# First mixer's attention: the multiplication of the softmax moves from VectorE to ScalarE

## The chip, the cores and the metric

The kernel runs on one NeuronCore of a Trainium2 chip. The metric is the device time of one execution in microseconds. The core has five engines that run their own instruction streams and wait for each other by semaphores: TensorE (PE; its weight loads are listed as PEld), VectorE (DVE), ScalarE (ACT), GpSimd (POOL) and SyncE (SP, which issues the transfers).

## The reference, cut to what matters

Two layers of an encoder, 256 tokens of 1024 channels, in float32. Each layer is a half-step SwiGLU block, a mixer, and another half-step SwiGLU block. The first layer's mixer projects the tokens once into 18 tiles of 128 channels: 12 go to a convolution branch (short convolution, gate, long convolution by Fourier transforms), 6 to a windowed attention with 8 query heads of 64 channels and 2 key/value heads. The attention's softmax has a sink logit in the denominator:

```
s = q @ k^T * D**-0.5 - slope * |distance|, masked outside the band
m = max(max(s), sink)
p = exp(s - m)
p = p / (sum(p) + exp(sink - m))
o = p @ v
```

Both branches are concatenated and go through one output projection. The second layer's mixer is a bidirectional RWKV-7 scan; it is not touched by the change.

## The kernel before, in words

Activations are kept channel-major: 128 channels on the partitions, 256 tokens along the free axis. All weights come as one stream of steps of three blocks of 128x1024, loaded by SyncE into two raw buffers. Each step is split into a high and a low part: ScalarE makes the high part (L187 and L193, `next_hi`), VectorE the low part of the first two blocks (L199, `next_lo`) and GpSimd that of the last block (L208). A product is three TensorE matmuls (L244 to L246).

The first mixer (`pe_mix0`, `act_mix0`, `dve_mix0`) is a hand-written loop over j = 0 to 17, one projected tile each. The order in which an engine's work stands in its own loop body is the order in which it runs; nothing is scheduled by a planner. Below, "step j" is one pass of that loop. A projected tile is brought out of PSUM by VectorE (L1099, `evacuate`); ScalarE then starts its short convolution (L1062) or squares it, and VectorE finishes the convolution in the next step (L1105 and L1107, `conv`). From j = 9 to 16 the attention runs beside it, one head per step, head h = j - 9:

- VectorE, `biased`: adds the distance bias to the scores (L1130), takes the row maximum (L1133) and its negative (L1135, which releases ScalarE);
- ScalarE, `exps`: two exponentials of 128x256, one per half of the queries, each with its row sum (L1028), and the exponential of the sink (L1029, which releases VectorE);
- VectorE, `shares`: the sum (L1140), its reciprocal (L1142), and the two multiplications of the exponentials by it (L1145, into the tile SC, which releases TensorE);
- TensorE, `probs`: four transposes of the shares (L895); ScalarE copies them out of PSUM (L1023) in the next step; TensorE multiplies them with the values for two heads at a time (L909), ScalarE copies the result (L1033) and VectorE makes its low part (L1150).

TensorE's own order in a step is: projection of tile j, for odd j from 11 the product with the values, the scores (L886: heads 0 and 1 in steps 8 and 9, then two heads at a time in steps 10, 12 and 14), the transposes of head j - 9, and for j = 9, 11, 13, 15 the transposes of a gated tile (L918). The scores of head 1 use a swapped copy of the keys, which ScalarE makes in step 9 (L1049). ScalarE's order in a step is: L1023, `exps`, then the step's single copies (L1049 or L1053), in steps 9, 12 and 15 the high part of the next weights (L187, L193), in odd steps from 11 the copy L1033, and last L1062. VectorE's order is: in even steps from 12 L1150, `biased`, `conv` of tile j - 1, `shares`, in steps 10, 13 and 16 the low part of the next weights (L199), and `evacuate` of tile j. GpSimd makes the low part of the third block and the gates of the convolution branch (L1941). After the transposes of the last head (step 16) TensorE does the two Fourier transforms (L925), the last projection and the output projection.

Of the kernel before, what the change touches and what calls it, by code (L numbers as in the profile page):

```python
# [95 lines left out]
def build(nc, io):  # L96
    fp32 = mybir.dt.float32
    f32r = mybir.dt.float32r
    ALU = mybir.AluOpType
    ACT = mybir.ActivationFunctionType  # L100
# [3 lines left out]
    with ctx:  # L104
# [3 lines left out]
        def sem(name):  # L108
            return ctx.enter_context(nc.semaphore(name))
# [33 lines left out]
        def pcol(name, i=0):  # L143
            return par[:, COL[name] + i:COL[name] + i + 1]
# [80 lines left out]
        def next_hi(act, s):  # L225
            if s < STEPS:
                split_hi(act, s)
# [157 lines left out]
        def act_squares(act):  # L385
            for a, b in ((0, 4), (4, 6), (6, 8)):
                nc.scalar.activation(XSQ[:, a:b, :], X[:, a:b, :], ACT.Square).then_inc(sq_ready, 1)

        def act_sqrt_table(act):
            nc.scalar.activation(small[:, 61:62], eps6[:, 0:1], ACT.Sqrt)  # L390
# [37 lines left out]
        def act_root(act, n):  # L428
            act.wait_ge(st_ready, n + 1)
            if n == 0:  # L430
                act.wait_ge(eps_ready, 1)
            nc.scalar.activation(std[:, :], stats_bank(n)[:, 0:L], ACT.Sqrt, bias=eps6[:, 0:1], scale=1.0 / C).then_inc(std_ready, 1)
# [160 lines left out]
        def place(n):  # L593
            at[0] += n
            assert at[0] <= ARENA
            return arena[:, at[0] - n:at[0]]
# [17 lines left out]
        SC = place(2 * 512).rearrange("p (o a k) -> p o a k", o=2, a=2)  # L614
        EX = place(2 * 512).rearrange("p (o a k) -> p o a k", o=2, a=2)
# [13 lines left out]
        amax, anegm, asum, aes, aden, arden = (small[:, 4 + 2 * k:6 + 2 * k] for k in range(6))  # L629
# [52 lines left out]
        sc_ready = sem("sc_ready")  # L682
        ex_ready = sem("ex_ready")
        pr_ready = sem("pr_ready")
        pt_done = sem("pt_done")
        vt_done, vt_ready, cz_ready = sem("vt_done"), sem("vt_ready"), sem("cz_ready")
        pt_ready = sem("pt_ready")
# [119 lines left out]
        def ub(j):  # L807
            return UB[2 if j == 2 else j % 2][:, 0:L]
# [192 lines left out]
        def u_home(j):  # L1001

            m = IN_ORDER[j]
            return U3[:, (j - 6) % 4, 1:L + 1] if m < 12 else UQ[:, m - 12, :]

        def act_mix0(act):
            A = nc.scalar.activation
            act_squares(act)
            next_hi(act, S_IN + 1)
            act_sqrt_table(act)  # L1010
            act.wait_ge(rest_full, 32)

            def first(j):
                act.wait_ge(blocks_done, 3 * S_IN + j + 1)
                A(u_home(j), ub(j), ACT.Copy).then_inc(first_copied, 1)
            first(0)
            first(1)
            act_root(act, 1)
            first(2)

            def probs(h):
                act.wait_ge(pt_done, h + 1)
                A(PT[:, h % 2, :, :], bank[5][:, :].rearrange("p (b q) -> p b q", b=2), ACT.Copy).then_inc(pt_ready, 1)  # L1023

            def exps(h):
                act.wait_ge(sc_ready, h + 1)
                for a in range(2):
                    A(EX[:, h % 2, a, :], SC[:, h % 2, a, :], ACT.Exp, bias=anegm[:, a:a + 1], accum_out=asum[:, a:a + 1])  # L1028
                A(aes, anegm, ACT.Exp, bias=pcol("sink", h)).then_inc(ex_ready, 1)  # L1029

            def values(t):
                act.wait_ge(pv_done, 2 * t + 2)
                A(AH[:, t, :], bank[2][:, 0:L], ACT.Copy).then_inc(mix_hh, 1)  # L1033

            for j in range(18):
                h = j - 8
                if 2 <= h:
                    probs(h - 2)
                if 1 <= h <= NQ:
                    exps(h - 1)  # L1040
                if j == 6:
                    act.wait_ge(ss_done, 1)
                    A(RN[:, 0, :], bank[3][0:16, 0:L], ACT.Sqrt, bias=eps6[0:16, 0:1], scale=1.0 / HD).then_inc(root_ready, 1)
                if j == 7:
                    act.wait_ge(vt_done, 1)
                    A(VT[:, :, :], bank[7][:, 0:2 * P].rearrange("p (a c) -> p a c", a=2), ACT.Copy).then_inc(vt_ready, 1)
                if j == 9:
                    act.wait_ge(ks_done, 1)
                    A(KN[:, 1, :], bank[7][:, 0:L], ACT.Copy).then_inc(ks_ready, 1)  # L1049
                if j in (10, 12, 14, 16):  # L1050
                    c = (j - 10) // 2
                    act.wait_ge(zt_done, c + 1)
                    A(ZT[:, :, c * P:(c + 1) * P], bank[3][:, 0:L].rearrange("p (a k) -> p a k", a=2), ACT.Copy)\  # L1053
                        .then_inc(zt_ready, 1)
                if j and j % 3 == 0:
                    next_hi(act, S_IN + j // 3 + 1)
                if h >= 3 and h % 2:
                    values((h - 3) // 2)
                act.wait_ge(u_ready, j + 1)
                m = IN_ORDER[j]  # L1060
                if m < 12:
                    A(UC[:, m, :], U3[:, (j - 6) % 4, 1:L + 1], ACT.Identity, bias=pcol("conv_b", m),  # L1062
                      scale=pcol("conv_w", 12 + m)).then_inc(cv_ready, 1)
                elif m < 17:
                    A(XSQ[:, m - 12, :], UQ[:, m - 12, :], ACT.Square).then_inc(qsq_ready, 1)
            next_hi(act, S_OUT + 1)
            next_hi(act, S_OUT + 2)
            for c in range(HT):
                act_mixed(act, c)

        def act_mixed(act, t, base=0):

            act.wait_ge(ym_ready, base + t + 1)
            nc.scalar.activation(HH[:, t, :], ymix[:, t % 2, :], ACT.Copy).then_inc(mix_hh, 1)
# [6 lines left out]
        def dve_mix0(dve, own):  # L1081
            tt, stt, ts = nc.vector.tensor_tensor, nc.vector.scalar_tensor_tensor, nc.vector.tensor_scalar
# [54 lines left out]
            def shares(h):  # L1137
                o = h % 2
                dve.wait_ge(ex_ready, h + 1)
                own(tt(aden, asum, aes, ALU.add))  # L1140
                own.settle()
                own(nc.vector.reciprocal(arden, aden))  # L1142
                own.settle()
                for a in range(2):
                    last = ts(SC[:, o, a, :], EX[:, o, a, :], arden[:, a:a + 1], None, ALU.mult)  # L1145
                last.then_inc(pr_ready, 1)

            def values(t):
                dve.wait_ge(mix_hh, t + 1)
# [16 lines left out]
            for j in range(18):  # L1166
                h = j - 8
                if j == 6:
                    dve.wait_ge(root_ready, 1)
                    nc.vector.reciprocal(RN[:, 1, :], RN[:, 0, :]).then_inc(rec_ready, 1)  # L1170
                if h >= 4 and h % 2 == 0:
                    values((h - 4) // 2)
                if 1 <= h <= NQ:
                    biased(h - 1)
                if j >= 7:
                    conv(j - 1)
                if 1 <= h <= NQ:
                    shares(h - 1)
                if j > 1 and j % 3 == 1:
                    next_lo(dve, S_IN + j // 3 + 1)  # L1180
                if j == 17:
                    times_filter(0)
                evacuate(j)
                if j == 7:
                    norm()
# [1313 lines left out]
        @block.scalar  # L2499
        def _(act):  # L2500
            act.wait_ge(eps_ready, 1)
            nc.scalar.activation(small[:, 60:61], eps6[:, 0:1], ACT.Sin)
            act_filter_sin(act, 0)
            next_hi(act, 0)
            act_filter_sin(act, 1)
            act_norm_in(act, 0, ("ffn1_norm", 0))
            act_squares(act)
            act_ffn(act, 0, S_FFN[0], 0)
            act_norm_in(act, 1, ("mix_norm", 0))
            act_mix0(act)  # L2510
            next_hi(act, S_OUT + 3)
            act_norm_in(act, 2, ("ffn2_norm", 0))
            act_ffn(act, 2, S_FFN[1], FT)
            act_norm_in(act, 3, ("ffn1_norm", CT))
            act_ffn(act, 3, S_FFN[2], 2 * FT)
            act_mix1(act)
            act_norm_in(act, 5, ("ffn2_norm", CT))
            act_ffn(act, 5, S_FFN[3], 3 * FT)
# [203 lines left out]
```

## Time and profile before

| | |
|---|---|
| median of 3 runs | 1245.34 us (1240.94 to 1245.88) |
| the profiled execution's own time | 1245.4 us |
| its span, first to last instruction | 1243.6 us |
| mean granted TensorE clock | 0.992 of full speed |
| PE busy | 1199.9 us (96%) |
| DVE busy | 803.9 us (65%) |
| ACT busy | 658.3 us (53%) |
| POOL busy | 404.0 us (32%) |

Busy time is the time in which an engine works on at least one instruction. The attention steps 9 to 16 lie between 255 and 302 us after the span's start. In a timeline a row is: start in us, duration in us, engine, line, operation, what it writes and reads, and in brackets how long the engine was idle before it and who ended that.

### The profile page before, as it was taken

Reading aid. Unit: us, or ns where it says so; the run is one execution under the profiler, and the core shown is the slowest. Engines: PE = TensorE matmul, PEld = TensorE weight load, DVE = VectorE, ACT = ScalarE, POOL = GpSimd, SP = SyncE. Lnnn points to the kernel's source line nnn. Section 1 sums busy time; section 2 is a strip of 40 time slices with the busy share of each in tenths; the row PEclk is TensorE's granted clock in tenths of the full one; section 3 lists DMA queues with packets and bytes.
Section 4 is the critical chain, followed back from the end, with each engine's and each line's share of the span. In section 5 each row is a group of like instructions: output and inputs, shape, how many; then the busy total and the mean of one; then the engine's idle time right before and its main releaser. Section 6 shows DMA issues by size and latency. Waiting matters only on the chain.

```text
span 1243.6 us, 27160 instructions
## 1 busy us (share of the span) xinstructions
PE 1199.9 (96%) x11086; PEld 1082.2 (87%) x11086; DVE 803.9 (65%) x1280; ACT 658.3 (53%) x1118; POOL 404.0 (32%) x218
## 2 busy tenths in 40 slices
PE   8999999988999999999999989998999999999998
PEld 5799999876889999989999979987999888899998
DVE  7755555788585555485555569869777657755554
ACT  5545444654274454474545546685666544554552
POOL 0343443312113434424344310015343412334433
PEclk9999999998999999999999989999999999999999
DMA  9355445422254454555545534411000015554452
GB/s 357 108 200 202 164 190 203 153 102 103 102 195 176 187 199 165 197 200 203 189 170 197 182 133 160 186 52 54 3 4 4 3 62 196 203 202 163 192 193 94
DMA packets 18656, 187.99 MB, mean 151 GB/s; under 512 B 2064, under 2 KB 2576, under 8 KB 3600
## 3 DMA queue, kind: packets, MB, share of 16 engines
q1 hardware_dynamic: 18576, 186.84, 41.1%
q8 instruction: 60, 0.98, 0.3%
q14 instruction: 20, 0.16, 0.0%
HBM read 185.78 MB, written 1.05 MB: 150 GB/s over the span
## 4 chain that ended last, share of the span: by engine, by line
PE 79%; DVE 13%; ACT 6%; issue 2%; DMA 0%; SPq 0%; POOL 0%; DVEq 0%
PE gu_bank L265 23%; PE gu_bank L267 12%; PE bank L244 7%; PE bank L246 7%; PE bank L245 7%; PE bank L1446 7%; PE gu_bank L244 3%; PE gu_bank L1446 3%; DVE WL L199 3%; PE gu_bank L245 3%; PE gu_bank L246 3%; ACT WH L187 2%; PE gu_bank L1477 2%; DVE HX L395 1%; PE bank L925 1%
## 5 line engine op out<-in xcount | busy, mean ns | idle before, releaser
L208 POOL TENSOR_TENSOR WL<-raw,WH 128x1024 fp32r<-128x1024 f32 x96 | 327.1, 3407 | 595.7 <-ACT WH L193 573.3
L265 PE MATMUL gu_bank<-HX,WH 128*128 128x512 f32 x1408 | 502.3, 399 | 7.3 <-DVE PL L531 4.6
L267 PE MATMUL gu_bank<-HX,WL 128*128 128x256 f32 x1408 | 395.2, 281 | 0.0
L199 DVE TENSOR_TENSOR WL<-raw,WH 128x2048 fp32r<-128x2048 f32 (+1 forms) x114 | 245.0, 2149 | 128.9 <-ACT WH L187 128.9
L265 PEld LDWEIGHTS gu_bank<-HX,WH 128*128 128x128 f32 x1408 | 264.7, 188 | 71.0 <-DVE PL L531 5.2
L267 PEld LDWEIGHTS gu_bank<-HX,WL 128*128 128x128 f32 x1408 | 266.1, 189 | 0.1
L187 ACT ACTIVATE WH<-raw 128x2048 fp32r<-128x2048 f32 (+1 forms) x114 | 205.1, 1799 | 23.8 <-PE gu_bank L246 14.4
L244 PE MATMUL bank<-PH,WH 128*128 128x256 f32 (+1 forms) x720 | 201.7, 284 | 1.0 <-ACT arena L2043 0.9
L245 PE MATMUL bank<-PL,WH 128*128 128x256 f32 (+1 forms) x720 | 201.6, 283 | 0.0
L246 PE MATMUL bank<-PH,WL 128*128 128x256 f32 (+1 forms) x720 | 201.5, 283 | 0.0
L452 ACT ACTIVATE work<-gu_bank 128x512 f32<-128x512 f32 x88 | 52.5, 597 | 168.1 <-PE gu_bank L267 168.1
L244 PEld LDWEIGHTS bank<-PH,WH 128*128 128x128 f32 (+1 forms) x720 | 135.4, 190 | 5.4 <-ACT arena L2043 1.4
L519 DVE TENSOR_TENSOR gu_bank<-gu_bank,work 128x512 f32<-128x512 f32 x84 | 58.8, 699 | 120.1 <-ACT work L452 119.4
L246 PEld LDWEIGHTS bank<-PH,WL 128*128 128x128 f32 (+1 forms) x720 | 135.6, 190 | 0.0
L245 PEld LDWEIGHTS bank<-PL,WH 128*128 128x128 f32 (+1 forms) x720 | 135.5, 190 | 0.0
L193 ACT ACTIVATE WH<-raw 128x1024 fp32r<-128x1024 f32 x114 | 119.4, 1047 | 0.0
L457 ACT ACTIVATE work<-gu_bank 128x256 f32<-128x256 f32 x84 | 32.2, 384 | 131.7 <-DVE gu_bank L526 131.7
L244 PE MATMUL gu_bank<-HX,WH 128*128 128x256 f32 x336 | 99.9, 297 | 1.3 <-DVE HX L395 1.1
L245 PE MATMUL gu_bank<-HX,WH 128*128 128x256 f32 x336 | 96.7, 288 | 0.0
L246 PE MATMUL gu_bank<-HX,WL 128*128 128x256 f32 x336 | 96.5, 287 | 0.0
L244 PEld LDWEIGHTS gu_bank<-HX,WH 128*128 128x128 f32 x336 | 66.2, 197 | 4.9 <-issue 3.3
L245 PEld LDWEIGHTS gu_bank<-HX,WH 128*128 128x128 f32 x336 | 66.2, 197 | 0.3 <-issue 0.2
(313 smaller groups left out, 1800.7 us busy)
## 6 DMA issues: line engine op xcount, KB each, us to landing
raw<-stream_in SPq DMA_DIRECT2D x114, 1536.0 KB, 6.5
cst<-const_in SPq DMA_DIRECT2D x1, 1568.0 KB, 17.5
X<-xT_in SPq DMA_DIRECT2D x1, 1024.0 KB, 6.2
raw<-stream_in SPq DMA_DIRECT2D x1, 1024.0 KB, 8.2
arena<-hconst_in SPq DMA_DIRECT2D x2, 512.0 KB, 11.5
out<-X SPq DMA_DIRECT2D x4, 256.0 KB, 2.1
arena<-hconst_in SPq DMA_DIRECT2D x1, 768.0 KB, 14.3
arena<-fw_in SPq DMA_DIRECT2D x1, 512.0 KB, 9.0
```

Of the source, the lines that this page charges most:

```text
L187: nc.scalar.activation(WH[:, slot, :cut], raw[:, slot, :cut], ACT.Copy).then_inc(hi_ready, 1)
L193: nc.scalar.activation(WH[:, slot, cut:end], raw[:, slot, cut:end], ACT.Copy).then_inc(hi_last, 1)
L199: nc.vector.tensor_tensor(WL[:, slot, :cut], raw[:, slot, :cut], WH[:, slot, :cut].bitcast(fp32), ALU.subtract).then_inc(lo_ready, 1)
L208: (eng or nc.gpsimd).tensor_tensor(WL[:, slot, cut:end], raw[:, slot, cut:end], WH[:, slot, cut:end].bitcast(fp32), ALU.subtract).then_inc ...
L244: nc.tensor.matmul(out_ap, wh, xh, start=start, stop=False, **kw)
L245: nc.tensor.matmul(out_ap, wh, xl, start=False, stop=False, **kw)
L246: return nc.tensor.matmul(out_ap, wl, xh, start=False, stop=stop, **kw)
L265: nc.tensor.matmul(out[:, :], WH[:, slot, w:w + P], HX[:, x, :, :].rearrange("p i t -> p (i t)"), start=k == 0, stop=False)
L267: return nc.tensor.matmul(out[:, L:2 * L], WL[:, slot, w:w + P], HH[:, x, :], start=False, stop=k == CT - 1)
L452: nc.scalar.activation(gus[o], gu_bank[:, o, :, L:2 * L], ACT.Copy).then_inc(gx_ready, 1)
L519: nc.vector.tensor_tensor(gated, gu_bank[:, o, :, 0:L], gus[o], ALU.add).then_inc(gsum_ready, 1)
L1446: last = nc.tensor.matmul(dst[r, cols], w[r], x[r], start=start, stop=stop)
```

## The change

The two multiplications of `shares` leave VectorE. VectorE keeps the sum and the reciprocal, and the reciprocal now raises a new semaphore, `den_ready`. ScalarE gets a function `shares(h)`, called directly behind `exps(h)`: it waits for `den_ready` and does the two multiplications as copies with a scale per partition, and its second one raises `pr_ready` for TensorE.

```diff
+        den_ready = sem("den_ready")
@@ act_mix0
+            def shares(h):
+                o = h % 2
+                act.wait_ge(den_ready, h + 1)
+                for a in range(2):
+                    last = A(SC[:, o, a, :], EX[:, o, a, :], ACT.Copy, scale=arden[:, a:a + 1])
+                last.then_inc(pr_ready, 1)
+
@@ act_mix0, the loop over j
                 if 1 <= h <= NQ:
                     exps(h - 1)
+                    shares(h - 1)
@@ dve_mix0, shares
                 own(tt(aden, asum, aes, ALU.add))
                 own.settle()
-                own(nc.vector.reciprocal(arden, aden))
-                own.settle()
-                for a in range(2):
-                    last = ts(SC[:, o, a, :], EX[:, o, a, :], arden[:, a:a + 1], None, ALU.mult)
-                last.then_inc(pr_ready, 1)
+                nc.vector.reciprocal(arden, aden).then_inc(den_ready, 1)
```

The new lines shift the numbers behind them: the multiplication is L1036 in the changed kernel, the exponentials L1029 and L1030, the copies L1058 (keys), L1062 (gated tile) and L1041 (values), the convolution's start L1071, the sum L1149 and the reciprocal L1151.

ScalarE's instructions in step 9 and at the start of step 10, in the kernel before (WH is the high part of the weights, small holds the maxima and sums):

```order
L1028 ACTIVATE arena,small<-arena,small 128x256 x2
L1029 ACTIVATE small<-small,par 128x2
L1049 ACTIVATE arena<-bank 128x256
L187 ACTIVATE WH<-raw 128x2048
L193 ACTIVATE WH<-raw 128x1024
L1062 ACTIVATE arena<-arena,par 128x256
L1023 ACTIVATE arena<-bank 128x512
```

The same place in the changed kernel, with what each waits for:

```order
L1029 ACTIVATE arena,small<-arena,small 128x256 [waits sc_ready]
L1029 ACTIVATE arena,small<-arena,small 128x256
L1030 ACTIVATE small<-small,par 128x2
L1036 ACTIVATE arena<-arena,small 128x256 [waits den_ready]
L1036 ACTIVATE arena<-arena,small 128x256
L1058 ACTIVATE arena<-bank 128x256 [waits ks_done]
L187 ACTIVATE WH<-raw 128x2048 [waits blocks_done,raw_full1]
L193 ACTIVATE WH<-raw 128x1024
L1071 ACTIVATE arena<-arena,par 128x256 [waits u_ready]
```

Two instructions and a wait now stand between the sink's exponential and the key copy and the high part of the weights.

ScalarE in steps 11 and 12 of the changed kernel (hx is the attention's result for the output projection):

```order
L1029 ACTIVATE arena,small<-arena,small 128x256 x2
L1030 ACTIVATE small<-small,par 128x2
L1036 ACTIVATE arena<-arena,small 128x256 x2
L1041 ACTIVATE hx_53<-gu_bank 128x256
L1071 ACTIVATE arena<-arena,par 128x256
L1024 ACTIVATE arena<-bank 128x512
L1029 ACTIVATE arena,small<-arena,small 128x256 x2
L1030 ACTIVATE small<-small,par 128x2
L1036 ACTIVATE arena<-arena,small 128x256 x2
L1062 ACTIVATE arena<-gu_bank 128x2x128
L187 ACTIVATE WH<-raw 128x2048
L193 ACTIVATE WH<-raw 128x1024
```

The copy of the values' result (L1041) and the next high part (L187) too stand behind the new pair.

VectorE at the end of step 9 and in step 10, in the kernel before:

```order
L1140 TENSOR_TENSOR small<-small 128x2
L1142 RECIPROCAL small<-small 128x2
L1145 TENSOR_SCALAR arena<-arena,small 128x256 x2
L1099 TENSOR_TENSOR arena<-gu_bank,rstd 128x256
L1130 SCALAR_TENSOR_TENSOR arena<-arena,bank 128x512
L1133 TENSOR_REDUCE small<-arena 128x2
L1135 TENSOR_SCALAR small<-small,par 128x2
L1105 SCALAR_TENSOR_TENSOR arena<-arena,par 128x256
L1107 SCALAR_TENSOR_TENSOR arena<-arena,par 128x256
L1140 TENSOR_TENSOR small<-small 128x2
L1142 RECIPROCAL small<-small 128x2
L1145 TENSOR_SCALAR arena<-arena,small 128x256 x2
```

In the changed kernel the two L1145 rows are gone, and nothing else of it has moved on VectorE.

## Rows read from the trace of the kernel before

**Rows 1.** The page's busy times: us, share of the span, instructions.
```profile
PE 1199.9 (96%) x11086; PEld 1082.2 (87%) x11086; DVE 803.9 (65%) x1280; ACT 658.3 (53%) x1118; POOL 404.0 (32%) x218
```

**Rows 2.** Waits between 255 and 305 us: who waited for whom, total, times, longest.
```profile
ACT arena L1062 <- DVE arena L1099: 18.3, 6, 4.7
PEld bank L895 <- DVE arena L1145: 11.2, 8, 2.8
```

**Rows 3.** ScalarE in step 9, timeline.
```profile
258.79 0.28 ACT L1029 ACTIVATE small<-small,par 128x2 f32<-128x2 f32 x1
258.98 0.36 ACT L1049 ACTIVATE arena<-bank 128x256 f32<-128x256 f32 x1
```

**Rows 4.** VectorE in steps 9 and 10, timeline.
```profile
259.11 0.16 DVE L1140 TENSOR_TENSOR small<-small 128x2 f32<-128x2 f32 x1 [0.45 <-ACT small L1029]
259.30 0.17 DVE L1142 RECIPROCAL small<-small 128x2 f32<-128x2 f32 x1
259.50 0.62 DVE L1145 TENSOR_SCALAR arena<-arena,small 128x256 f32<-128x256 f32 x2
260.03 0.42 DVE L1099 TENSOR_TENSOR arena<-gu_bank,rstd 128x256 f32<-128x256 f32 x1
260.56 0.69 DVE L1130 SCALAR_TENSOR_TENSOR arena<-arena,bank 128x512 f32<-128x512 f32 x1
...
265.67 0.91 DVE L1145 TENSOR_SCALAR arena<-arena,small 128x256 f32<-128x256 f32 x2
266.50 2.28 DVE L199 TENSOR_TENSOR WL<-raw,WH 128x2048 fp32r<-128x2048 f32 x1
```

**Rows 5.** ScalarE: scaled copies SBUF to SBUF; the convolution's start.
```profile
343.51 1.69 ACT L382 ACTIVATE HX<-X,par 128x256 fp32r<-128x256 f32 x4
346.64 0.91 ACT L382 ACTIVATE HX<-X,par 128x256 fp32r<-128x256 f32 x2 [1.44 <-DVE X L998]
...
297.34 0.59 ACT L1062 ACTIVATE arena<-arena,par 128x256 f32<-128x256 f32 x1
```

**Rows 6.** GpSimd's gate in step 10, timeline.
```profile
265.45 0.72 POOL L1941 TENSOR_TENSOR arena<-arena 128x256 f32<-128x256 f32 x1 [0.88 <-DVE arena L1107]
```

**Rows 7.** TensorE: scores L886 and transposes L895, steps 9 to 16.
```profile
259.39 1.13 PE L886 MATMUL bank<-arena 64*128 64x256 f32 x4 [0.29 <-ACT arena L1049]
...
273.11 0.66 PE L895 MATMUL bank<-cst,arena 128*128 128x128 f32 x4 [1.73 <-DVE arena L1145]
...
276.78 1.13 PE L886 MATMUL bank<-arena 64*128 64x256 f32 x8
...
284.22 0.74 PE L895 MATMUL bank<-cst,arena 128*128 128x128 f32 x4 [1.85 <-DVE arena L1145]
...
289.42 1.13 PE L886 MATMUL bank<-arena 64*128 64x256 f32 x8
...
302.09 1.12 PE L895 MATMUL bank<-cst,arena 128*128 128x128 f32 x4 [2.63 <-DVE arena L1145]
```

**Rows 8.** Steps 11 to 13: the copy of the values' result, its user; convolution.
```profile
271.91 0.36 ACT L1033 ACTIVATE hx<-gu_bank 128x256 fp32r<-128x256 f32 x1
...
273.30 0.42 DVE L1150 TENSOR_TENSOR hx<-gu_bank,hx 128x256 fp32r<-128x256 f32 x1
...
280.15 2.23 DVE L1105 SCALAR_TENSOR_TENSOR arena<-arena,par 128x256 f32<-128x256 f32 x1 [0.52 <-ACT arena L1062]
```

**Rows 9.** VectorE in steps 14 to 16.
```profile
291.45 0.68 DVE L1130 SCALAR_TENSOR_TENSOR arena<-arena,bank 128x512 f32<-128x512 f32 x1
...
297.47 0.42 DVE L1150 TENSOR_TENSOR hx<-gu_bank,hx 128x256 fp32r<-128x256 f32 x1 [1.67 <-ACT hx L1033]
```

**Rows 10.** Stretches: their length, PE, PEld, DVE, ACT, POOL busy (instructions), granted clock.
```profile
262.00:268.00 6.00, 4.62 (x39) 4.04 (x38) 5.51 (x8) 2.50 (x9) 3.12 (x2) 1.00 0.02 4
...
282.50:284.00 1.50, 0.00 (x0) 0.00 (x0) 1.43 (x5) 0.30 (x1) 0.46 (x1) 1.00 0.00 0
...
285.50:287.00 1.50, 1.50 (x9) 1.50 (x9) 1.50 (x4) 0.26 (x1) 0.00 (x0) 0.50 0.04 11
```

## The prediction, made before the changed kernel had run

> **What bounds the kernel now.** I began with the page: TensorE is busy for 96% of the span, VectorE for 65%, ScalarE for 53% [rows 1]. That says nothing of the touched steps, so I followed the chain of waits through 255 to 302 us and read the timeline of each engine there. In these steps TensorE is not the bound: its transposes L895 waited for the multiplication L1145 in every one of the eight steps, 11.2 us in sum [rows 2]. ScalarE seems to have room: it waited 18.3 us for L1099, six times [rows 2]. But that room lies only at the ends of steps without the high part of weights. The end of the stage is set by one instruction, the transposes of the last head at 302.09, to which TensorE came 2.63 us early [rows 7]; behind it stands only TensorE work (Fourier transforms, projections), for which VectorE and ScalarE then wait. So the question is by how much 302.09 moves, and all that follows moves with it.
>
> **The parts and their prices.** Removed from VectorE: a pair of L1145 starts at 259.50 and the next instruction at 260.03, so 0.53 us a step [rows 4]. In step 10 the pair occupies 265.67 to 266.50, 0.83 us. Nothing else leaves.
>
> Added to ScalarE: two copies with a scale per partition, SBUF to SBUF, 128x256. The nearest rows are L382, the same form: two take 0.91 us and four 1.69, so one more costs (1.69 - 0.91) / 2 = 0.39, one is 0.52 long, and the next instruction can start after 0.78 [rows 5]. From below the price is bounded by the copy L1049, which comes out of PSUM and is 0.36 long [rows 3]; from above by L1062, with scale and bias, 0.59 long [rows 5]. I take L382, the same form. No row shows the new handshake; each of its halves has a neighbour. The sink's exponential ends at 259.07 and VectorE starts L1140 at 259.11; the reciprocal ends 0.36 after L1140's start [rows 3, 4]. With 0.04 for the way back the new pair starts at 259.51 and ScalarE's next instruction at 260.29, where now it stands at 258.98: **ScalarE's followers are 1.31 us later in each step, of which 0.53 is waiting**. TensorE's transposes: now released 1.01 after L1140's start (0.39 + 0.62), then 0.36 + 0.04 + 0.91 = 1.31, so **0.30 later** per head. With copies 0.16 shorter (L1049) the two are 0.99 and about 0, with copies 0.07 longer (L1062) 1.45 and 0.44. The table of functions need not be loaded again: the copies L1049 and L1033 already follow the exponentials without a load.
>
> What is queued behind the new wait on ScalarE differs by step, and that decides the sum:
>
> Step 9. Behind it stands the key copy L1049, for which TensorE's scores of head 1 wait (0.29 idle) [rows 7], and for these VectorE's L1130 at 260.56: its evacuation L1099 would already let it go at about 260.4 [rows 4]. So VectorE's saving of 0.53 is worth nothing here and L1130 starts 1.31 later. The high part L187 and with it GpSimd's L208 and the convolution's L1062 and L1105 move by the same 1.31.
>
> Step 10. +1.31 up to the reciprocal. Then 0.83 is saved, but the low part L199 moves up to directly behind the reciprocal: it would start at 266.98, while GpSimd's gate L1941 (at 265.45, 0.72 long [rows 6], now 1.31 later) runs until 267.48. The L1145 pair at 265.67, inside L1941, took 0.91 instead of 0.62 [rows 4, 6]. By that pair (0.29 lost, 0.50 of L1941 left) I charge L199 with 0.30. The Trainium skill (SBUF — State Buffer, "Who interferes with whom") says that VectorE and GpSimd share a port pair under an exclusive lock, that a VectorE instruction with two SBUF inputs is held by a GpSimd one that reads SBUF, and that ScalarE never waits for anyone. The long L1145 pair agrees. By that rule the multiplication is safer on ScalarE and L199, with two SBUF inputs, is the one held; without the rule the sum would be 0.3 smaller. Step 10's evacuation: 1.31 - 0.83 + 0.30 = +0.78.
>
> Step 11. exps +0.78. ScalarE's copy L1033 (now 271.91) stands behind the new pair: +2.09, so it ends at 274.36, and VectorE's L1150, now at 273.30 with 0.99 of slack behind that copy, starts at 274.40: +1.10 [rows 8]. The saved 0.53 turns into waiting.
>
> Step 12. exps +1.10, the high part L187 +1.10 + 1.31 = +2.41, and with it L1062 and the convolution L1105 of step 13, which today already waits 0.52 for it and then is 2.23 long beside GpSimd's part of the same weights [rows 8]. Both move together, so it stays as long: +2.41.
>
> Step 13. The saving of 0.53 counts, for VectorE goes on to L199: +1.88 at the evacuation. But the transposes of head 4 go to 284.22 + 2.41 + 0.30, +2.71 [rows 7].
>
> Step 14. VectorE alone would be at +1.35 (another 0.53 saved). Its L1130 for head 6 needs the scores that TensorE begins at 289.42 and ends at 290.55; these follow the transposes of head 4 and a projection, part of it at the lower clock [rows 10], so they end 2.71 later, at 293.26, and L1130 starts at 293.30 instead of 291.45: +1.85 [rows 7, 9].
>
> Step 15. Behind the new pair stand the high part and the copy L1033; VectorE waits for it 1.67 us already today [rows 9]. +1.85 + 1.31 = +3.16 for L1150 and for everything of step 16.
>
> Step 16. +3.16 and the 0.30 of the handshake: the transposes start 3.46 us later, at 305.55. The copy L1053 of the gated tile, which the Fourier transforms need, falls behind the pair too, but ends during the transposes (1.12 long [rows 7]), so it costs nothing; without that cover it would be some 0.3. The weights' transfers start up to 3 us later here, and no part of the stage shows a wait for one; I cost them at nothing.
>
> **Sum: +3.5 us.** The profiled execution took 1245.4 us with a span of 1243.6, so a like one would take 1248.9. It lies 0.1 above the median of the runs, 1245.34, so the median comes out at 1248.8. With the low price the same walk gives 0.99 - 0.53 = 0.46 at steps 10 to 12, 1.45 for the high part of step 12 and for the scores of step 14, where L1130 comes out at +0.6, and 0.6 + 0.99 = +1.6 at the end. With the high one it gives 0.92, then 0.92 + 1.45 - 0.99 = 1.38, 2.83, 3.27 at the scores, 2.41 at L1130, and 2.41 + 1.45 + 0.44 = +4.3. The forecast's own range is thus 1246.9 to 1249.6 about 1248.8.
>
> **Rivals.** First, TensorE's clock falls in more places (chance 0.18). The granted clock is 1.00 in 282.5 to 284.0, where TensorE does nothing, and 0.50 (1.2 GHz instead of 2.4) in 285.5 to 287.0 [rows 10]; the last transposes, behind 2.63 us of idling, take 1.12 instead of 0.66 [rows 7]. The change makes the idling longer: 1.6 us instead of 0.29 before the scores of head 1, about 2.8 instead of 1.85 before the transposes of head 4, about 3.7 instead of 2.63 before the last ones. From transposes to scores TensorE took 276.78 - 273.11 = 3.67 us in step 12 and 289.42 - 284.22 = 5.20 with the same work and the lower clock between steps 13 and 14 [rows 7], so a further fall costs up to 1.53. Two of them on the path and twice the 0.46 at the last transposes, for the slow stretch goes on beyond them, give 3.5 + 3.06 + 0.9 = +7.5, or 1252.8. This one ends on the other side: slower by more than can be told from no change. It decides from the point at which TensorE's idling in steps 9 to 12, 1.73 us at the longest today and followed by full-speed work (0.66 for the transposes), reaches the 1.85 behind which the clock fell [rows 7]. Against it: by the walk it is 1.6 us at most there. The Trainium skill (TensorE: Matmul & The Clock Gate, "HAM oscillation") warns that idle gaps put the array back to half its clock, each time anew; the fall in rows 10 agrees. By it alone each of the three gaps that grow could cost 1.53, 4.6 on top of the sum.
>
> Second, VectorE is the bound in all steps (0.10). For it: VectorE is busy for 5.51 of the 6 us from 262 [rows 10], and ScalarE idles 18.3 us [rows 2]. Then 8 x 0.53 are saved and 0.30 lost: -3.9, or 1241.4. Against it: VectorE's waits for ScalarE at 280.15 and 297.47 [rows 8, 9], both just behind a step with a high part.
>
> Third, the delays of steps 9 and 11 are covered (0.12), because the key copy or the values' copy comes earlier than the walk says. Then VectorE gains 0.83 + 0.53 by step 12, the high part of step 12 takes back 1.31, steps 13 and 14 save 1.06, and step 15 and the handshake cost 1.61: +0.5, or 1245.8. Against it: both copies have a definite place behind the pair, and L1049 has a waiter today.
>
> **How the numbers follow.** The forecast has 0.60. 0.5% is 6.2 us, about what a measurement of this kernel can tell from no change; the three runs of before lie 4.9 apart. Slower than 1251.6 takes most of the first rival, 0.14, and 0.04 for the forecast's upper edge with scatter: 0.18. Faster than 1239.1 takes only the second rival's tail: 0.03. The rest, 0.79, is no change that can be told. The range goes from 1243.0, between the second and third rivals, to 1253.5, just beyond the first.
>
> **What the profile would show.** L1036 pairs of about 0.91, each starting some 0.45 behind the sink's exponential; idle time before L1036 charged to the reciprocal; the scores of head 1 waiting for the key copy about 1.6 us instead of 0.29; L1150 of step 12 waiting for ScalarE, which today it does not; L1105 of step 13 at about 282.6; the last transposes at about 305.5; L1145's 0.53 gone from VectorE without a shorter stage. I am wrong if the last transposes start before 302, if the pair takes under 0.6 or over 1.2 us, or if the clock is below 1.00 in stretches between 256 and 284.

## The result, and the profile after

| | before | changed |
|---|---|---|
| median, the first comparison | 1241.95 us (6 runs, 1240.94 to 1245.88) | 1249.21 us (6 runs, 1246.88 to 1251.92) |
| ratio, 95% interval | | 1.0048 [1.0035, 1.0061] |
| median, a second comparison | 1243.71 us (31 runs) | 1249.23 us (7 runs) |
| ratio, 95% interval | | 1.0040 [1.0025, 1.0056] |
| profiled execution, span | 1245.4 us, 1243.6 | 1246.9 us, 1245.1 |
| its mean granted clock | 0.992 | 0.993 |

By the two ratios the change costs 5 to 6 us (the medians differ by 7.3 and 5.5). The forecast was 3.5. The two profiled executions alone differ by 1.5 us; that is no measure of the change: they differ by 2.57 us already at the first exponential (257.79 and 255.22), in stretches that the change does not touch. So in what follows times inside the attention are counted from the first exponential of the same execution, and "the stretch" is from there to the last transposes: **44.30 us before** (257.79 to 302.09), **47.78 after** (255.22 to 303.00), +3.48.

The waits between 252 and 305 us in the changed kernel, of the same view as [rows 2]:

```profile
PEld bank L896 <- ACT arena L1036: 12.8, 7, 4.2
...
ACT arena L1071 <- DVE arena L1108: 7.5, 4, 2.9
ACT arena L1036 <- DVE small L1151: 6.0, 8, 1.7
...
DVE hx L1155 <- ACT hx L1041: 4.2, 2, 3.3
DVE arena L1139 <- PE bank L887: 3.8, 4, 2.1
DVE arena L1114 <- ACT arena L1071: 2.3, 2, 1.9
```

ScalarE's idling at the end of the steps fell from 18.3 to 7.5 us. But another 6.0 us is now waiting for the reciprocal in the middle of the steps, and VectorE waits for ScalarE and for TensorE's scores at places where it hardly did.

The timeline of the changed kernel in step 9, ScalarE, VectorE and TensorE, which answers to [rows 3, 4, 7]:

```profile
256.22 0.28 ACT L1030 ACTIVATE small<-small,par 128x2 f32<-128x2 f32 x1
256.93 0.91 ACT L1036 ACTIVATE arena<-arena,small 128x256 f32<-128x256 f32 x2 [0.43 <-DVE small L1151]
257.74 0.36 ACT L1058 ACTIVATE arena<-bank 128x256 f32<-128x256 f32 x1
...
256.54 0.16 DVE L1149 TENSOR_TENSOR small<-small 128x2 f32<-128x2 f32 x1 [0.44 <-ACT small L1030]
256.73 0.17 DVE L1151 RECIPROCAL small<-small 128x2 f32<-128x2 f32 x1
256.81 0.40 DVE L1108 TENSOR_TENSOR arena<-gu_bank,rstd 128x256 f32<-128x256 f32 x1
259.32 0.69 DVE L1139 SCALAR_TENSOR_TENSOR arena<-arena,bank 128x512 f32<-128x512 f32 x1 [2.10 <-PE bank L887]
...
258.16 1.13 PE L887 MATMUL bank<-arena 64*128 64x256 f32 x4 [1.61 <-ACT arena L1058]
```

From the sink's exponential to the key copy it is now 1.52 us instead of 0.19: 1.33 later, forecast 1.31. The pair takes 0.91, as L382 did. TensorE's scores of head 1 wait 1.61 instead of 0.29, and VectorE, which is done early, waits 2.10 for them.

Later steps, VectorE and TensorE, with what each waits for; they answer to [rows 4, 7, 8, 9]:

```profile
264.32 2.76 DVE L199 TENSOR_TENSOR WL<-raw,WH 128x2048 fp32r<-128x2048 f32 x1
...
271.94 0.42 DVE L1155 TENSOR_TENSOR hx<-gu_bank,hx 128x256 fp32r<-128x256 f32 x1 [0.92 <-ACT hx L1041]
...
280.14 2.19 DVE L1114 SCALAR_TENSOR_TENSOR arena<-arena,par 128x256 f32<-128x256 f32 x1 [1.92 <-ACT arena L1071]
...
290.74 0.69 DVE L1139 SCALAR_TENSOR_TENSOR arena<-arena,bank 128x512 f32<-128x512 f32 x1 [0.58 <-PE bank L887]
...
298.11 0.42 DVE L1155 TENSOR_TENSOR hx<-gu_bank,hx 128x256 fp32r<-128x256 f32 x1 [3.29 <-ACT hx L1041]
...
284.46 1.12 PE L896 MATMUL bank<-cst,arena 128*128 128x128 f32 x4 [2.74 <-ACT arena L1036]
...
303.00 1.12 PE L896 MATMUL bank<-cst,arena 128*128 128x128 f32 x4 [3.96 <-ACT arena L1036]
```

Each of the forecast waits is there: the values' copy in step 12 (0.92), the convolution in step 13 (1.92 instead of 0.52), the scores in step 14 (0.58), the values' copy in step 16 (3.29 instead of 1.67). TensorE's idling before the last transposes rose from 2.63 to 3.96 us.

What the forecast's walk through the steps did not have is TensorE's clock behind them. Stretches of the changed kernel, with the columns of [rows 10]:

```profile
299.05:303.00 3.95, 0.00 (x0) 0.00 (x1) 3.37 (x8) 2.25 (x9) 1.22 (x1) 0.78 0.00 0
303.00:308.40 5.40, 5.40 (x10) 2.79 (x11) 2.50 (x4) 1.30 (x3) 0.00 (x0) 0.53 0.59 200
308.50:311.00 2.50, 2.50 (x17) 1.95 (x16) 1.37 (x3) 0.00 (x0) 0.00 (x0) 1.00 0.43 182
```

TensorE idles for 3.95 us, the clock falls to its lower level (1.2 GHz) in that time, and stays there for most of the next 5.4 us. From the last transposes to the first matmul of the inverse Fourier transform (L976 before, L977 after) it is 21.55 us before and 22.56 after: 1.0 more.

### The profile page after: what moved, and what is told of

It reads as the page before. It is cut to its first block, busy times and chain, and to the rows that moved or that the text cites. A ratio compares the mean times of both kernels' runs of the same rounds, so it can differ in the third digit from the quotient of the medians.

```text
span 1245.1 us, 27160 instructions
## 1 busy us (share of the span) xinstructions
PE 1195.7 (96%) x11086; PEld 1077.6 (87%) x11086; DVE 799.3 (64%) x1264; ACT 665.2 (53%) x1134; POOL 404.0 (32%) x218
## 4 chain that ended last, share of the span: by engine, by line
PE 79%; DVE 13%; ACT 6%; issue 2%; DMA 1%; SPq 0%; POOL 0%; DVEq 0%
PE gu_bank L265 23%; PE gu_bank L267 12%; PE bank L244 7%; PE bank L246 7%; PE bank L245 7%; PE bank L1451 7%; PE gu_bank L244 3%; PE gu_bank L1451 3%; PE gu_bank L245 3%; PE gu_bank L246 3%; DVE WL L199 2%; ACT WH L187 2%; PE gu_bank L1482 2%; DVE HX L395 1%; PE bank L926 1%
## 5 line engine op out<-in xcount | busy, mean ns | idle before, releaser
L199 DVE TENSOR_TENSOR WL<-raw,WH 128x2048 fp32r<-128x2048 f32 (+1 forms) x114 | 245.5, 2154 | 128.9 <-ACT WH L187 128.9
L187 ACT ACTIVATE WH<-raw 128x2048 fp32r<-128x2048 f32 (+1 forms) x114 | 205.1, 1799 | 23.1 <-PE gu_bank L246 14.4
```

The costliest lines, as they stand in the source:

```text
L187: nc.scalar.activation(WH[:, slot, :cut], raw[:, slot, :cut], ACT.Copy).then_inc(hi_ready, 1)
L199: nc.vector.tensor_tensor(WL[:, slot, :cut], raw[:, slot, :cut], WH[:, slot, :cut].bitcast(fp32), ALU.subtract).then_inc(lo_ready, 1)
```

## The experiments

Two explanations stand against each other. The order theory says that the change costs what stands behind the new pair in ScalarE's order. The clock theory says that a good part of the cost is a lower TensorE clock, brought on by TensorE's longer waits. Each was written down with the numbers that it gives before a kernel ran.

Times are medians, the ratio is to the kernel before in the same comparison. "Stretch" and "tail" come from one profile of each kernel: the stretch is as above, the tail is from the last transposes to the first inverse-transform matmul, where the instructions are the same in all kernels; it is 20.06 or 20.07 us where the clock is full behind the last transposes, and longer where it falls there. "Clock" is the mean over a kernel's executions.

| kernel | time, us | ratio, 95% interval | stretch | tail | clock (executions) |
|---|---|---|---|---|---|
| before, again | 1243.23 | 0.9994 [0.9982, 1.0005] | 44.37 | 20.06 | 0.9916 (12) |
| changed, again | 1249.23 | 1.0040 [1.0025, 1.0056] | 48.22 | 21.47 | 0.9883 (7) |
| changed, two fills | 1247.31 | 1.0028 [1.0013, 1.0042] | 47.38 | 20.06 | 0.9918 (11) |
| before, two fills | 1243.96 | 0.9996 [0.9986, 1.0007] | 44.67 | 20.06 | 0.9923 (12) |
| changed, three fills | 1246.39 | 1.0027 [1.0014, 1.0040] | 47.34 | 20.07 | 0.9920 (12) |
| extra work on ScalarE | 1246.67 | 1.0027 [1.0014, 1.0041] | 46.66 | 21.69 | 0.9927 (10) |
| no multiplication | 1240.21 | 0.9973 [0.9960, 0.9986] | 41.20 | 20.06 | 0.9929 (10) |
| copies ahead of the pair | 1245.02 | 1.0017 [1.0000, 1.0035] | 47.05 | 21.77 | 0.9914 (10) |
| pair on ScalarE in two steps | 1243.45 | 1.0000 [0.9987, 1.0012] | 43.41 | 20.07 | 0.9914 (12) |
| evacuation ahead of the shares | 1243.36 | 1.0004 [0.9992, 1.0016] | 44.11 | 20.06 | 0.9927 (12) |
| both of the last two | 1244.61 | 1.0012 [1.0001, 1.0024] | 44.81 | 20.07 | 0.9922 (12) |

The two kernels themselves were run again first, for the scatter and for the clock of each execution.

> The kernel before, unchanged, as a measured kernel, for the granted clock of each of its executions. Order theory (the change costs by what stands behind the new pair on ScalarE): ratio 1.000; the stretch from the first exponential to the last transposes stays at 44.3 us (257.79 to 302.09 in the first profile) to 0.3. Clock theory (a good part of the 0.5% is that TensorE's clock falls more often in the changed kernel): its executions lie at a mean clock of 0.992 to 0.994, above the 0.986 to 0.989 of five of six executions of the changed kernel.

> The changed kernel, unchanged. Both theories: ratio 1.003 to 1.006. Order theory: the stretch from the first exponential (255.22) to the last transposes (303.00) is 47.8 us again, 3.5 above before. Clock theory: in a profile at a clock of 0.989 there are slow stretches inside the attention steps that the first profile of it (0.993) does not have.

The stretch of the kernel before is 44.37, as expected. Its tail is 20.06 instead of 21.55: in this execution the clock did not fall at the last transposes, though nothing was filled. Its mean clock is 0.9916, lower than the clock theory had said (0.992 to 0.994), but above the changed kernel's 0.9890 in the first comparison and 0.9883 in this. The second profile of the changed kernel (clock 0.987) shows a fall in step 9, which the first does not have (its clock is 1.00 from 256 to 284 us). TensorE there, in the timeline:

```profile
259.11 1.73 PE L887 MATMUL bank<-arena 64*128 64x256 f32 x4 [1.62 <-ACT arena L1058]
260.77 1.11 PE L896 MATMUL bank<-cst,arena 128*128 128x128 f32 x4
```

And the stretches around it, columns as in [rows 10]:

```profile
258.00:259.50 1.50, 0.39 (x2) 0.36 (x3) 0.17 (x1) 1.50 (x4) 0.00 (x0) 1.00 0.00 0
259.50:261.00 1.50, 1.50 (x5) 0.76 (x4) 0.12 (x1) 1.50 (x2) 0.00 (x0) 0.50 0.00 0
```

Behind the same wait of 1.6 us the clock held in the first profile and fell in the second; the scores take 1.73 instead of 1.13 us. The second exponentials come 8.15 us behind the first here and 6.51 there. Most of it is absorbed later: this stretch is 48.22, 0.44 longer.

**Fills.** Extra matmuls whose result nobody uses keep TensorE busy where it waits longest:

```diff
+                for _ in range({13: 5, 16: 8}.get(j, 0)):
+                    nc.tensor.matmul(bank[7][:, 0:L], ident, dist[:, 0, :], start=True, stop=True)
                 if 1 <= h <= NQ:
                     probs(h - 1)
```

> The changed kernel with idle TensorE time filled: 5 extra matmuls of 128x256 (some 0.45 us each, result unused) ahead of the transposes of head 4 (step 13) and 8 ahead of the last transposes (step 16). Order theory: the fill leaves TensorE free before the pair ends, so the order of things stays; what returns is only the slow clock: no fall at 284 (1.1 us shorter to the scores of step 14, of which VectorE passes on 0.5 to 0.6) and none at 302 (the last transposes 0.66 instead of 1.12, the Fourier transforms behind them 3.5 instead of 5.1): in all 2.5 us shorter than the changed kernel, ratio to before about 1.002. Clock theory: more than that, 4 us or more, ratio 1.001 or below. If the pair's wait is shorter than thought, TensorE comes late and it is slower than the changed kernel.

> The kernel before with the same kind of fill in the same two places, 3 and 5 extra matmuls (its waits are shorter). Order theory: VectorE bounds step 14 here, so only the last slow stretch returns, 0.46 at the transposes and 1.0 at the transforms: 1.4 us faster, ratio 0.9988, and the difference between the two filled kernels is what the order alone costs, 3.0 us (3.5 less the 0.5 that the slow projection adds in the changed kernel). Clock theory: the two filled kernels differ by less than 2 us.

The end of the stretch with the fill, in the changed kernel (L951 is the fill):

```profile
301.39 3.61 PE L951 MATMUL bank<-arena,cst 128*128 128x256 f32 x16
305.09 0.66 PE L896 MATMUL bank<-cst,arena 128*128 128x128 f32 x4
305.58 3.60 PE L926 MATMUL bank<-arena 128*128 128x512 f32 x8
```

The transposes take 0.66 instead of 1.12 and the Fourier matmuls 3.60 instead of the 5.68 of the first profile. The mean clock of the changed kernel rises to 0.9918, which is that of the kernel before (0.9915 over 31 executions), and its mean time falls from 1249.6 (13 executions) to 1247.35: 2.3 us, near the 2.5 expected. The scatter of the executions leaves 0.8 to 3.8 for it (95%), so the 4 of the clock theory lies just outside. A second way to the same number needs no fill: among the 95 executions of the kernel before in three comparisons, 0.001 less of mean clock goes with 0.73 us more, and the changed kernel's clock is 0.0029 lower, which makes 2.1 us. With the clock evened out, 3.5 us (2.1 to 4.9) remain to the 1243.84 mean of the kernel before, and 3.8 to the filled one; the order theory said 3.0, the clock theory less than 2. The profiles give 3.0 (47.38 against 44.37) and 2.7 (against 44.67).

The fill does not help the kernel before: its mean is 0.2 us lower, with an interval from 1.3 lower to 0.8 higher, against the expectation of 1.4. The second profile of that kernel shows one reason: without a fill its last transposes already ran at full clock (tail 20.06), so there is nothing to give back in such an execution. In the filled one's profile the clock falls elsewhere, in step 12 (stretch, columns as in [rows 10]):

```profile
270.00:276.00 6.00, 4.77 (x28) 4.78 (x29) 4.93 (x15) 4.03 (x11) 0.00 (x0) 0.72 0.40 170
```

Whether that is how the gain is lost in most of its executions, one profile does not show.

> The changed kernel with three fills: 2 extra matmuls ahead of the scores of head 1 (step 9), 5 and 8 ahead of the transposes in steps 13 and 16. If the fall of the clock in step 9 that one of the two profiles of the changed kernel shows comes of the 1.6 us wait there, its mean clock rises above the 0.9918 of the kernel with two fills and it is up to 0.8 us faster than that (half of its executions having the fall, 1.6 us each). If that fall has nothing to do with the wait: as the kernel with two fills, 1247.3. Order theory: it does not come below before plus 3.0 us, since the order is the same.

Two more matmuls ahead of the scores of step 9. Mean 1246.91 us against 1243.35 for before (+3.6), clock 0.9920 against 0.9918 with two fills. A gain over two fills is not shown: 1.0027 and 1.0028. But its profile has no fall at all (granted clock 1.00 from 254 to 314 us), and its stretch is still 47.34: 3.0 above before. That is nearly the cost of the order with the clock taken out of it.

**ScalarE's part alone.** VectorE keeps the multiplications; ScalarE does a pair of the same kind on constants, into a tile that nobody reads (the wait is for its own last pair, long done):

```diff
                 A(aes, anegm, ACT.Exp, bias=pcol("sink", h)).then_inc(ex_ready, 1)
+                if h:
+                    act.wait_ge(px_done, 2 * h)
+                for a in range(2):
+                    A(PX[:, a, :], dist[:, a, :], ACT.Copy, scale=pcol("sink", h)).then_inc(px_done, 1)
```

> The kernel before, the multiplications left on VectorE, with two more scaled copies of 128x256 on ScalarE directly behind the sink's exponential (constants into an unused tile, nothing waits for them): the moved work alone, without the wait for the reciprocal and without VectorE's saving. Order theory: 0.78 at each of the three places where a waited-for instruction stands behind it (steps 9, 12, 15): from the first exponential to the last transposes 44.3 + 2.3 = 46.6 us. Clock theory: under 0.8 us here, since the waits on TensorE grow little. A theory that ScalarE has room (it idles 18 us): 44.3.

The first exponentials and the last transposes of its profile:

```profile
257.19 0.51 ACT L1030 ACTIVATE arena<-arena,small 128x256 f32<-128x256 f32 x1 [0.37 <-DVE small L1141]
...
303.85 1.11 PE L897 MATMUL bank<-cst,arena 128*128 128x128 f32 x4 [3.42 <-DVE arena L1151]
```

303.85 - 257.19 = 46.66, expected 46.6. It comes in three jumps: against before, the first exponentials of heads 1, 4 and 7 are 0.79, 1.59 and 2.36 later, and nothing is added between. Each of these follows a step (9, 12, 15) in which the high part of the weights stands behind the pair. So 0.78 us of work on an engine that idles 18 us costs three times 0.78. The theory that ScalarE has room falls.

**VectorE's part alone.** The multiplications are left out, so the shares are not divided by their sum; the transposes read the exponentials (EX instead of SC, not shown in the cut):

```diff
-                own(nc.vector.reciprocal(arden, aden))
-                own.settle()
-                for a in range(2):
-                    last = ts(SC[:, o, a, :], EX[:, o, a, :], arden[:, a:a + 1], None, ALU.mult)
-                last.then_inc(pr_ready, 1)
+                nc.vector.reciprocal(arden, aden).then_inc(pr_ready, 1)
```

> The kernel before without the two multiplications (the shares are not divided by their sum; the transposes read the exponentials and are released by the reciprocal): what VectorE's saving is worth at most. Order theory: nothing in step 9 (the scores of head 1 come last), about 0.4 in step 10 (the low part of the weights is held by GpSimd's gate), 0.53 in each of steps 11, 13 and 14, and 0.64 at the last transposes: 41.7 us from the first exponential to the last transposes. VectorE-bound theory: 8 x 0.53 + 0.1 less, 39.9.

The same two rows in its profile:

```profile
256.12 0.51 ACT L1028 ACTIVATE arena<-arena,small 128x256 f32<-128x256 f32 x1 [0.37 <-DVE small L1135]
...
297.32 0.66 PE L895 MATMUL bank<-cst,arena 128*128 128x128 f32 x4 [1.98 <-DVE small L1142]
```

41.20: the work taken from VectorE is worth 3.1 us when nothing is given to ScalarE, 0.5 more than expected, and not 4.3. The VectorE-bound theory falls: the exponentials of heads 1, 4 and 7, behind the steps with a high part, gain nothing, and the other places gain 0.46, 0.66, 0.67, 0.66 and 0.65. The 0.5 has its row above: in the changed kernel the evacuation starts 0.08 behind the reciprocal's start (256.73, 256.81), where the multiplication started 0.20 behind it [rows 4], because VectorE no longer waits for its own reciprocal. So a step saves 0.53 + 0.12 = 0.65, as those gains show.

**Order alone.** The pair stays on ScalarE, behind the key copy in step 9 and the values' copy in step 11, which is taken out of its later place (cut here):

```diff
                     exps(h - 1)
-                    shares(h - 1)
@@ behind the key copy
+                if j == 11:
+                    values(0)
+                if 1 <= h <= NQ:
+                    shares(h - 1)
```

> The changed kernel with two of ScalarE's copies ahead of the pair: the key copy in step 9 and the values' copy in step 11; the high parts of the weights stay behind it. Order theory: 1.0 us back of 3.5, 46.8 from the first exponential to the last transposes; the scores of head 1 wait 0.3 as before, and VectorE does not wait for the values' copy in step 12. If the handshake itself were the cost, the place would not matter: 47.8.

47.05 instead of the 46.8 expected, and 47.78 of the changed kernel. The copy in step 9 is in time, as expected, and the scores of head 1 wait 0.29 again. But that returns little: the exponentials of head 1 come 6.24 us behind the first ones, against 6.51 in the changed kernel and 5.17 before. The timeline of the kernel before shows why, the row maximum's negative on VectorE and what ScalarE does meanwhile:

```profile
262.00 0.23 DVE L1135 TENSOR_SCALAR small<-small,par 128x2 f32<-128x2 f32 x1
...
261.99 0.59 ACT L1062 ACTIVATE arena<-arena,par 128x256 f32<-128x256 f32 x1
262.48 0.58 ACT L1023 ACTIVATE arena<-bank 128x512 f32<-128x512 f32 x1
262.96 0.50 ACT L1028 ACTIVATE arena<-arena,small 128x256 f32<-128x256 f32 x1
```

The maxima are there at 262.23, but ScalarE, late from the high part of the weights, comes to the exponentials only at 262.96. So the scores had 0.73 us to spare already before, and it is the high part behind the pair that moves step 10, not the key copy.

In step 11 the expectation was missed: VectorE still waits for the values' copy, now since TensorE's product comes late (timeline of ScalarE):

```profile
272.29 0.38 ACT L1041 ACTIVATE hx<-gu_bank 128x256 fp32r<-128x256 f32 x1 [1.20 <-PE gu_bank L910]
```

Its stretches before that:

```profile
264.00:267.00 3.00, 0.83 (x5) 0.83 (x6) 2.93 (x5) 1.18 (x3) 0.83 (x2) 0.89 0.00 0
267.00:270.00 3.00, 3.00 (x17) 3.00 (x17) 2.93 (x6) 1.28 (x3) 0.00 (x0) 0.54 0.32 79
```

The clock fell there in this execution. That the place of the pair matters is suggested by its ratio (1.0017 against 1.0040), but the two intervals overlap; the kernel that follows shows it better.

**The pair on ScalarE only where nothing that is waited for stands behind it**, in steps 10 and 14. In the other six VectorE does it as before (cut here):

```diff
+        ON_VECTOR = (9, 11, 12, 13, 15, 16)
-                    shares(h - 1)
+                    if j not in ON_VECTOR:
+                        shares(h - 1)
```

> The multiplications on ScalarE in steps 10 and 14 alone, where no high part of weights and no waited-for copy stands behind them, and on VectorE in the other six. Order theory: 0.4 saved in step 10, 0.53 in step 14, nothing lost: 43.4 us from the first exponential to the last transposes, 0.9 below before; ratio 0.9993, too little to be told from the runs. If each move costs by itself, 44.3 or more.

The same two rows in its profile:

```profile
255.76 0.51 ACT L1030 ACTIVATE arena<-arena,small 128x256 f32<-128x256 f32 x1 [0.37 <-DVE small L1146]
...
299.17 0.66 PE L897 MATMUL bank<-cst,arena 128*128 128x128 f32 x4 [1.92 <-DVE arena L1159]
```

43.41, expected 43.4; the runs cannot tell it from before, as expected. Two handshakes and two pairs on ScalarE cost nothing where nothing waited for stands behind them.

**A version to beat both?** VectorE's 0.44 us of waiting for the sink's exponential might hold the evacuation, which then leaves its later place in steps 10 to 16. It is tried alone and together with the pair on ScalarE in steps 10 and 14:

```diff
+                if 2 <= h <= NQ:
+                    evacuate(j)
                 if 1 <= h <= NQ:
                     shares(h - 1)
```

> The kernel before with the multiplications where they were; VectorE's evacuation of the projected tile stands ahead of its shares in steps 10 to 16 instead of behind them, where it fills the 0.44 us in which VectorE waits for the sink's exponential. Order theory: 0.33 saved in each of steps 11, 13 (nothing, its wait lies elsewhere), 14 and 15 or 16, and ScalarE's L1062 is free of the low part of the weights: 43.4 us or less from the first exponential to the last transposes, 0.9 or more below before; ratio 0.998 to 0.9995. If the tile is not yet projected at that place, VectorE waits and it is no faster.

> Both together: the multiplications on ScalarE in steps 10 and 14 alone, the evacuation ahead of the shares in steps 10 to 16. Order theory: the two savings add up where both end at VectorE, 42.4 to 42.8 us from the first exponential to the last transposes, ratio 0.9985 or below; that would be the version faster than both kernels. If TensorE's order bounds it by then, it equals the better one of the two.

Both missed. At the new place the projection is not always done; VectorE in step 15 of the first of the two:

```profile
292.70 0.42 DVE L1099 TENSOR_TENSOR arena<-gu_bank,rstd 128x256 f32<-128x256 f32 x1 [1.13 <-PE gu_bank L246]
```

44.11 and 44.81 against the 43.4 and 42.4 to 42.8 expected: VectorE waits for TensorE's projection as soon as it asks for the tile earlier, and both together (1.0012 [1.0001, 1.0024]) are if anything slower than before. No version that does the whole softmax is shown to be faster than the kernel before.

## Why the prediction was right, and where it was short

The result, 1249.21, lies 0.4 from the forecast of 1248.8. Part of that is luck: the forecast added 3.5 to the 1245.34 of the first three runs of before, and with more runs its median is 1242 to 1244. A start that lay too high and a shift that came out too small cancel. The shift itself was forecast at 3.5 and is 5 to 6 (ratios 1.0048 and 1.0040). The forecast had called 6.2 us about the least that can be told from no change. The intervals are finer than that: the first, [1.0035, 1.0061], begins at 4.3 us. The slowdown is real, though smaller than 6.2.

- **ScalarE's followers 1.31 us later in each step.** 1.33 measured in step 9, the pair 0.91 as taken. The extra-work kernel shows the 0.78 of work in it by itself. The rest, 0.55, is the handshake: 0.43 of idle time in front of the pair, 0.09 by which the key copy before started ahead of the end of the sink's exponential [rows 3], and 0.03 more behind the pair.
- **The walk by steps.** The shifts of the exponentials of heads 1, 2, 3, 5, 6 and 7 against before, from the first exponential, in the first profile of the changed kernel: +1.34, +0.87, +1.22, +1.85, +1.87, +3.19; forecast +1.31, +0.78, +1.10, +1.88, +1.85, +3.16. Head 4 is at +2.55; the forecast had +2.41 for the high part in front of it. The last transposes: +3.48, forecast +3.46. The places that decide are the three high parts of weights (steps 9, 12 and 15, +1.34, +1.33 and +1.32) and, with 0.35, the values' copy in step 11. The forecast named these, but led with the key copy in step 9. The copy is late as forecast and its waiter waits, yet the kernel with the copy in time gets back only 0.27 of the 1.34.
- **The saving on VectorE.** Mis-sized: 0.65 a step, not 0.53. It counts only behind steps without a high part, and hardly shows in the walk.
- **GpSimd's gate and L199.** Charged with 0.30; L199 took 2.76 instead of 2.28, so 0.48. The direction was right: L199 was the one held, and the gate took 0.72 as before. In the second profile of the changed kernel L199 starts behind the gate's end and takes 2.27. In step 10 the 0.18 more and the larger saving of 0.12 nearly cancel.
- **The clock.** This is the term that the sum had wrong. It charged TensorE's clock with nothing new and set all of it aside as a rival at +7.5 with a chance of 0.18. It is neither: the two longest waits filled, the mean falls by 2.3 us (0.8 to 3.8) and the clock rises from 0.9886 to 0.9918, that of before. So the shift of 5 to 6 us is about 3.5 us of order (3.0 in the profiles) and about 2.3 us of clock. The rival's mechanism was right, its size was not: only some executions have a further fall on the path (step 9 in one of two profiles), and much of what it costs is absorbed by the next wait. Its condition fails: it wanted an idle time of 1.85 us in the early steps, and 1.62 was enough in one execution and not in another. The prediction's own sign of being wrong, a clock below 1.00 between 256 and 284 us, is missing in the first profile and there in the second (0.50 from 259.5 to 261).
- **The VectorE-bound rival** is excluded by the kernel without the multiplication (3.1 us, not 4.3). **The covered-delays rival** is excluded by the shifts of heads 1 and 3 (+1.34, +1.22) and by the 0.92 that L1155 waits.

What stays open: where the clock falls in most executions, and why there. Between 254 and 314 us the two profiles of the kernel before have two falls (from 284 and 301) and one (from 290), those of the changed kernel two (from 284 and 301) and three (from 259, 286 and 303), those of the changed kernel with two and three fills one (from 274) and none. That fits a fall more often in the changed kernel, but the counts are too small for a share. The 0.5 us or so between the 3.0 of the profiles and the 3.5 of the runs lies inside the scatter.

## What to carry to other kernels

In a lockstep of several engines, do not judge a move by the idle time of the engine that receives the work: list what stands behind the new instruction in that engine's order, and count the delay once for each that holds up the next step. Here 1.3 us three times, absorbed in part between, made 3.5, while 18 us of idle time lay at the ends of other steps. A waiter alone does not make such a place: the scores waited for the key copy, but the next exponentials were held by ScalarE's own queue 0.73 us longer. A handshake in the middle of an engine's step costs its wait as well as its work, and where it lengthens TensorE's idling it can be paid a second time in the clock, here with about 2 us.

## What the runs showed of the hardware beside that

The same program with the same wait of 1.6 us kept its clock in one execution and lost it in another (step 9, 1.13 and 1.73 us for the same scores), so single executions of one kernel differ: the 31 of before lie between 1240.91 and 1247.32 us at mean clocks of 0.986 to 0.995. A difference of 3 us between two profiles says nothing until both are aligned at the place of the change. Where the transforms ran at full clock the tail is 20.06 or 20.07 us, in eight profiles of eight kernels. The length of an idle time alone did not tell whether the clock falls: behind the 2.47 us in front of head 4's transposes it stayed at 1.00 in the profile of the extra-work kernel, behind 1.62 us in step 9 it fell in the second profile of the changed kernel.
